# Ten modulation slices of the first attention, accumulated on GpSimd and not on VectorE

## The chip, the core and the metric

One core of a Trainium2 chip. The time is the device time of one execution in microseconds. A core has TensorE (matmuls and transposes, into PSUM), VectorE, ScalarE and GpSimd (elementwise work), and SyncE, whose queue issues the DMA transfers here. Each engine works through its own instructions in order; they meet at semaphores.

## What is computed

A decoder trunk of two layers on 512 positions of width 1024, float32. Layer 0 mixes positions with a forgetting attention of 16 heads, layer 1 with a latent attention; a gated MLP with a short convolution follows each. Every one of the four sub-layers is modulated by a vector c:

```python
def ada_modulation(c, w, b):
    mod = jax.nn.silu(c) @ w + b            # w: 1024 x 3072
    shift, scale, gate = jnp.split(mod[:, None, :], 3, axis=-1)
    return shift, scale, gate
...
    shift, scale, gate = ada_modulation(c, ada_w[i, 0], ada_b[i, 0])
    h = rms_norm(x) * (1.0 + scale) + shift
    ...
    x = x + gate * y
```

The change concerns silu(c) @ w alone, for the gate of sub-layer 0 and the shift and scale of sub-layer 1.

## The kernel before

**Products.** Activations lie transposed: a tile has 128 features on partitions and 512 positions in the row. A weight block of 128 output features is loaded to raw (8 x 128 columns), one of two slots. To keep float32 accuracy it is split: ScalarE copies it to wh in a reduced format (L711), VectorE subtracts to get the rest, wl (L1134). A product is then 24 matmuls of 512 columns (L1679): high times high, low times high, high times low, for 8 blocks of depth, into one of two PSUM banks pj. SyncE loads the next block of a slot when L1134 has read the one before (slot_free, L483). A bank is free for TensorE when both ScalarE and VectorE have taken the result that it held (bank_free).

**Head pairs.** The first attention goes over 8 pairs of heads. Steps are numbered i, w: i = 0 to 3, w = 0 to 7, each i two pairs, each pair four steps d = w mod 4, one for each block of 128 queries, with d + 1 blocks of keys. In a step TensorE makes the scores of both heads (L1918 to L1924), then a part of the next pair's q, k and v products as filling, transposes the probabilities of the step before (L1934), and fills again; v is transposed once a pair (L2027), and at d = 0 the pair before is weighted (L1962). VectorE takes the row maxima (L1297), ScalarE the exponentials (L861, into tmp or diag), VectorE the reciprocals (L1305) and the normalisation (L1307). The scores of a step wait for the exponentials of the step before, since they use the same two banks sc. Behind that VectorE has: at d = 0 the split of one block and a half of v's copy (L1276), which frees the bank in which the k product starts six matmuls into the next step; at d = 1 the copy of v's transposes (L1326), the low part of the pair's output (L1312), a split and the low part of q (L1265); at d = 2 a split and the low part of k (L1271). In the last i the pairs run out, w = 4 to 7 have less filling, taken from the output projection.

**Modulation.** The vector-matrix product is done row by row: partitions hold rows of w, each is multiplied by its silu(c), and slices of rows are added up; a matmul with ones sums over partitions in the end (ada_sum, L1799 and L1802). A slice p is 1 MB, 2048 columns on 128 partitions of ada_w_sb, which has two halves used in turn. ADA is the list of slices: 0 to 3 are the gate of sub-layer 0 (each with two row blocks of 1024 columns and two values of c), 4 to 11 the shift and scale of sub-layer 1. The load of slice p (L499) overwrites slice p - 2 and waits until slice p - 1 has been added to it (ada_acc); after a sum it waits for the sum. Its place in SyncE's queue is written by hand (FOX_ADA_LOAD, FOXO_ADA_LOAD). The accumulation, ada_step, is one instruction of VectorE for 2048 columns, or two for 1024: multiply by c and add the slice before (L1175), or multiply alone for the first of a sum (L1177). Its place in VectorE's order is the table FOX_ADA, in which n is 8 i + w: slices 0 to 9 stand behind the steps n = 3, 7, 10, 12, 15, 19, 22, 24, 27 and 31. Slices 10 and 11 stand in the output projection. The gate's sum is taken by TensorE at i = 1, w = 6, the other in the output projection.

**GpSimd** builds constants at the start and then has nothing until 671 us, where it works out shift sums for the second layer (L680, L685).

Of the kernel before, what the change touches and what calls it, by code (L numbers as in the profile page):

```python
# [10 lines left out]
ALU = mybir.AluOpType  # L11
# [69 lines left out]
GK = AW // D  # L81
# [4 lines left out]
ADA = tuple((is_gate, k, g, DT // GK if is_gate else DT) for is_gate, k in ADA_GROUPS  # L86
            for g in range(DT // GK if is_gate else DT))
ADA_END = tuple(sum(DT // GK if is_gate else DT for is_gate, _ in ADA_GROUPS[:n + 1])
                for n in range(len(ADA_GROUPS)))
ADA_OUT = {0: ADA_END[1] - 2, 3: ADA_END[1] - 1}  # L90
# [7 lines left out]
LAST_FILL = (0, 4, 8, 11, 14, 17, 19, 20, 21, 22, 24, 33)  # L98
MLA_FILL = (0, 3, 7, 11, 15, 18, 21, 33, 33)
OUT_SUM = {5: 1}  # L100
FOX_ADA = {(n // 8, n % 8): p for p, n in enumerate((3, 7, 10, 12, 15, 19, 22, 24, 27, 31))}
FOX_ADA_LOAD = {(0, 5): 2, (1, 2): 3, (1, 3): 4, (1, 5): 5, (2, 2): 6, (2, 5): 7}
FOXO_ADA_LOAD = {0: 8, 2: 9, 3: 10, 4: 11}

# [35 lines left out]
def build(nc, x, c, ada_w, ada_b, fox_w_in, fox_b_f, fox_w_o, mla_w_a, mla_g_q, mla_g_kv,  # L140
# [7 lines left out]
    with ExitStack() as ctx:  # L148
        def sb(name, shape, dt):
            return ctx.enter_context(nc.sbuf_tensor(name, shape, dt))  # L150

        def sem(name):
            return ctx.enter_context(nc.semaphore(name))
# [19 lines left out]
        ada_w_sb = sb("ada_w_sb", [P, 2, AW], F32)  # L173
# [12 lines left out]
        csil = sb("csil", [P, DT], F32)  # L186
# [165 lines left out]
        x_e = sem("x_e")  # L352
        ada_in = [sem(f"ada_in{i}") for i in range(2)]
        ada_used = sem("ada_used")
        ada_acc = sem("ada_acc")
        ada0_in = [sem(f"ada0_in{i}") for i in range(BLOCKS)]
        f_in = sem("f_in")
# [93 lines left out]
        def ada_tiles(p):  # L451
            return ada_w_sb[:, p % 2, :].rearrange("p (t n) -> p t n", n=D)
# [194 lines left out]
        def _(pool):  # L647
# [19 lines left out]
            for part, row0 in enumerate((0, 32, HD + 1, HD + 33)):  # L667
                pool.wait_ge(pc, 7 + part)
                pool.affine_select(out=sel[:, :, :], in_=flags, compare_op=ALU.not_equal, fill=1.0,
                                   base=-row0, pattern=[[-2, PAIRS], [0, P]], channel_multiplier=1  # L670
                                   ).then_inc(pc, 1)

            def shift_sum(n0, side, k):

# [451 lines left out]
        def _(dve):  # L1126
# [38 lines left out]
            def ada_step(p):  # L1165

                is_gate, k, g, _ = ADA[p]
                dve.wait_ge(ada_in[p % 2], 16 * (p // 2 + 1))
                if g:
                    dve.wait_ge(ada_acc, p)  # L1170
                for t in range(GK if is_gate else 1):
                    w, was = [ada_tiles(q)[:, t, :] if is_gate else ada_w_sb[:, q % 2, :] for q in (p, p - 1)]
                    c_col = csil[:, g * GK + t:g * GK + t + 1] if is_gate else csil[:, g:g + 1]
                    if g:
                        ins = dve.scalar_tensor_tensor(out=w, in0=w, scalar=c_col, in1=was, op0=ALU.mult, op1=ALU.add)  # L1175
                    else:
                        ins = dve.tensor_scalar(w, w, c_col, None, ALU.mult)  # L1177
                ins.then_inc(ada_acc, 1)
# [160 lines left out]
            last = PAIRS // 2 - 1  # L1339
            for i in range(last):  # L1340
                for w in range(8):
                    fox_step(i, w, True, None)
                    if (i, w) in FOX_ADA:
                        ada_step(FOX_ADA[i, w])
            for w in range(9):
                fox_step(last, w, w < 4, 6 * last)
                if (last, w) in FOX_ADA:
                    ada_step(FOX_ADA[last, w])

            def xtile(m):  # L1350
                return xT[:, m, :] if isinstance(m, int) else xT[:, bass.ds(m, 1), :]
# [292 lines left out]
            last = HEADS // 2 - 1  # L1644
# [609 lines left out]
```

## Time and profile before

| | before |
|---|---|
| median of 3 runs | 1299.44 us (1298.76 to 1301.04) |
| the profiled execution | 1300.4 us |
| its span, first to last instruction | 1298.2 us |
| mean granted TensorE clock | 0.989 |
| TensorE busy | 1259.0 us (97%) |
| VectorE busy | 847.2 us (65%) |
| ScalarE busy | 540.2 us (42%) |
| GpSimd busy | 30.8 us (2%) |

The head pairs run from about 62 to 263 us. A busy share is an average over stages; what an edit is worth is read from the place where it stands. In a timeline a row has its start and its duration in us; "[0.68 <-ACT diag L861]" says that the engine sat idle 0.68 us before it and that line 861 of ScalarE released it.

### The profile page before, as it was taken

What the parts mean: (1) busy time and instruction counts of PE and PEld (TensorE: products, weight loads), DVE (VectorE), ACT (ScalarE), POOL (GpSimd) and SP (SyncE); (2) the same over time, 40 slices, a digit from 0 to 9 for tenths busy, and PEclk for the clock granted to TensorE, in tenths of its full rate; (3) what the DMA queues carried; (4) which work ended last, traced back from release to release, by engine and by line L of the source; (5) the groups of instructions that cost most, each with busy time, mean ns of one, the idle gap of its engine ahead of it and who ended that gap; (6) DMA issues with size and microseconds to landing.
All of it is one profiled execution on the core that took longest, in us unless ns stands there. A gap on an engine that the chain in (4) does not pass through costs nothing.

```text
span 1298.2 us, 17924 instructions
## 1 busy us (share of the span) xinstructions
PE 1259.0 (97%) x6179; PEld 984.7 (76%) x6179; DVE 847.2 (65%) x1284; ACT 540.2 (42%) x983; POOL 30.8 (2%) x39
## 2 busy tenths in 40 slices
PE   5999999999999999999999999999999999999997
PEld 3677777676888878888888666667788888888886
DVE  3656756766888888855547767765776666664332
ACT  5544444534333333332235566664543333332222
POOL 2000000000000000000020000000300000000000
PEclk8999999999999999999999999999999999999998
DMA  9623433342566656556532111123233333333332
GB/s 308 192 66 97 139 101 107 111 146 49 195 195 195 195 188 194 168 165 209 164 98 60 38 34 36 34 59 93 70 102 95 97 96 96 97 93 105 90 90 93
DMA packets 241012, 154.42 MB, mean 119 GB/s; under 512 B 38153, under 2 KB 232174, under 8 KB 237882
## 3 DMA queue, kind: packets, MB, share of 16 engines
q1 hardware_dynamic: 240954, 153.63, 39.6%
q8 instruction: 38, 0.62, 0.2%
q14 instruction: 20, 0.16, 0.0%
HBM read 151.47 MB, written 2.14 MB: 118 GB/s over the span
## 4 chain that ended last, share of the span: by engine, by line
PE 87%; DVE 6%; ACT 2%; SPq 2%; issue 1%; DMA 1%; POOL 0%; DVEq 0%; ACTq 0%; POOLq 0%
PE pj L1679 74%; PE ov L1962 3%; PE sc L1906 3%; PE tr L1934 3%; PE sc L1918 1%; DVE wl L1134 1%; SPq L530 1%; DVE tmp L1228 1%; ACT wh L711 1%; DMA first_ada<-in_ada_w_dram 1%; DVE nmax L1297 1%; PE ov L1847 1%; DVE hl L1209 0%; PE sc L1924 0%; ACT tmp L861 0%
## 5 line engine op out<-in xcount | busy, mean ns | idle before, releaser
L1134 DVE TENSOR_TENSOR wl<-raw,wh 128x1024 fp32r<-128x1024 f32 (+2 forms) x214 | 236.1, 1103 | 264.2 <-ACT wh L711 261.0
L711 ACT ACTIVATE wh<-raw 128x1024 fp32r<-128x1024 f32 (+2 forms) x214 | 204.4, 955 | 456.8 <-PE pj L1679 456.8
L1679 PE MATMUL pj<-hh,wh 128*128 128x512 f32 x944 | 377.0, 399 | 6.4 <-issue 3.1
L1679 PE MATMUL pj<-hh,wl 128*128 128x512 f32 x944 | 368.2, 390 | 0.0
L1679 PE MATMUL pj<-hl,wh 128*128 128x512 f32 x944 | 367.8, 390 | 0.0
L1679 PE MATMUL pj<-gh,wh 128*128 128x512 f32 x560 | 223.0, 398 | 1.1 <-DVE rope_sb L1597 0.5
L1679 PE MATMUL pj<-gh,wl 128*128 128x512 f32 x560 | 219.3, 392 | 0.0
L1679 PE MATMUL pj<-gl,wh 128*128 128x512 f32 x560 | 218.7, 391 | 0.0
L1679 PEld LDWEIGHTS pj<-hh,wh 128*128 128x128 f32 x944 | 177.4, 188 | 48.7 <-issue 10.2
L1679 PEld LDWEIGHTS pj<-hh,wl 128*128 128x128 f32 x944 | 177.3, 188 | 37.8
L1679 PEld LDWEIGHTS pj<-hl,wh 128*128 128x128 f32 x944 | 177.6, 188 | 33.6 <-DVE hl L1209 0.2
L1679 PEld LDWEIGHTS pj<-gh,wh 128*128 128x128 f32 x560 | 105.5, 188 | 27.7 <-issue 6.0
L1679 PEld LDWEIGHTS pj<-gh,wl 128*128 128x128 f32 x560 | 105.3, 188 | 22.1
L1679 PEld LDWEIGHTS pj<-gl,wh 128*128 128x128 f32 x560 | 105.4, 188 | 20.1
L1297 DVE TENSOR_REDUCE nmax<-sc 128x1 f32<-128x128 f32 (+3 forms) x128 | 59.4, 485 | 43.4 <-PE sc L1907 27.2
L861 ACT ACTIVATE tmp<-sc,nmax 128x128 f32<-128x128 f32 (+2 forms) x96 | 46.7, 488 | 94.9 <-DVE nmax L1297 94.9
L1175 DVE SCALAR_TENSOR_TENSOR ada_w_sb<-ada_w_sb,csil 128x1024 f32<-128x1024 f32 (+1 forms) x45 | 78.9, 1776 | 0.0
L868 ACT ACTIVATE soft<-tr 128x128 f32<-128x128 f32 (+3 forms) x128 | 52.5, 438 | 63.0 <-PE tr L1934 62.2
L1433 DVE SCALAR_TENSOR_TENSOR tmp<-pj,conv,tmp 128x510 f32<-128x510 f32 x84 | 62.9, 748 | 7.0 <-DVE tmp L1430 1.4
L967 ACT ACTIVATE tmp<-pj,conv 128x512 f32<-128x512 f32 x84 | 64.0, 762 | 0.0
L1430 DVE SCALAR_TENSOR_TENSOR tmp<-pj,conv,tmp 128x511 f32<-128x511 f32 x84 | 62.5, 744 | 0.0
L1906 PE MATMUL sc<-soft 128*128 128x128 f32 (+3 forms) x128 | 47.1, 449 | 0.9 <-DVE soft L1606 0.7
(216 smaller groups left out, 1048.2 us busy)
## 6 DMA issues: line engine op xcount, KB each, us to landing
raw<-in_ffn_w_in_dram SPq DMA_DIRECT2D x88, 512.0 KB, 3.8
ada_w_sb<-in_ada_w_dram SPq DMA_DIRECT2D x40, 1024.0 KB, 5.2
raw<-in_ffn_w_out_dram SPq DMA_DIRECT2D x32, 448.0 KB, 3.4
raw<-in_fox_w_in_dram SPq DMA_DIRECT2D x24, 512.0 KB, 3.8
first_ada<-in_ada_w_dram SPq DMA_DIRECT2D x16, 512.0 KB, 8.9
raw<-in_ffn_w_out_dram SPq DMA_DIRECT2D x16, 512.0 KB, 3.6
raw<-in_fox_w_o_dram SPq DMA_DIRECT2D x8, 512.0 KB, 3.7
raw<-in_mla_w_o_dram SPq DMA_DIRECT2D x8, 512.0 KB, 3.7
```

What stands on the lines that cost most here:

```text
L711: act.activation(wh[:, n0 % 2, 0:kt, :], raw[:, n0 % 2, 0:kt, :], ACT.Copy).then_inc(w_hi, 1)
L861: act.activation(prob[u % 4][:, 0:nc_], SC[u % 2][:, 0:nc_], ACT.Exp, bias=nmax[:, u % 8:u % 8 + 1], accum_out=rsum[:, u % 8:u % 8 + 1]).t ...
L868: act.activation(pt32(h, b), TR[bk][:, 0:(b + 1) * P].rearrange("p (k q) -> p k q", q=P), ACT.Copy).then_inc(p_out, 1)
L967: act.activation(y, PJ[(T + j) % 2][:, :], ACT.Identity, bias=ccol(l, 3, f), scale=ccol(l, 2, f)).then_inc(ev_a, 1)
L1134: dve.tensor_tensor(wl[:, n0 % 2, 0:kt, :], raw[:, n0 % 2, 0:kt, :], f32(wh[:, n0 % 2, 0:kt, :]), ALU.subtract).then_inc(w_lo, 1)
L1175: ins = dve.scalar_tensor_tensor(out=w, in0=w, scalar=c_col, in1=was, op0=ALU.mult, op1=ALU.add)
L1297: dve.tensor_reduce(nmax[:, u % 8:u % 8 + 1], SC[u % 2][:, 0:nc_], AX.X, ALU.max, negate=True).then_inc(nmax_s, 1)
L1430: dve.scalar_tensor_tensor(out=y[:, 1:S], in0=bk[:, 0:S - 1], scalar=ccol(l, 1, f), in1=y[:, 1:S], op0=ALU.mult, op1=ALU.add).then_inc(tap, 1)
L1433: dve.scalar_tensor_tensor(out=y[:, 2:S], in0=bk[:, 0:S - 2], scalar=ccol(l, 0, f), in1=y[:, 2:S], op0=ALU.mult, op1=ALU.add).then_inc(ev_ ...
L1679: ins = pe.matmul(bank_[:, :], (wl if term == 2 else wh)[:, s, kt, :], (rl if term == 1 else rh)(kt), start=start and j == 0, stop=stop an ...
L1906: pe.matmul(sc, q32(par)[:, q], k32(par)[:, 0:nc_], start=True, stop=False)
L1934: ins = pe.transpose(TR[bk][:, kb * P:(kb + 1) * P] if h == 0 else TR[bk][:, (b - kb) * P:(b - kb + 1) * P], prob[u % 4][:, kb * P:(kb + 1 ...
```

## The change

The table FOX_ADA and its calls of ada_step are gone from VectorE. GpSimd has a loop over slices 0 to 9 right behind its constants. For each it waits for the slice to land, multiplies it in place (one instruction, or two of 1024 columns), waits for that to be finished and for the slice before, and adds that one in a second instruction. The semaphores to SyncE and TensorE are the same. Slices 10 and 11 and all later ones stay with VectorE.

```diff
-FOX_ADA = {(n // 8, n % 8): p for p, n in enumerate((3, 7, 10, 12, 15, 19, 22, 24, 27, 31))}
...
+        ada_mul = sem("ada_mul")
...
+            def ada_slice(p):
+
+                is_gate, k, g, _ = ADA[p]
+                pool.wait_ge(ada_in[p % 2], 16 * (p // 2 + 1))
+                for t in range(GK if is_gate else 1):
+                    w = ada_tiles(p)[:, t, :] if is_gate else ada_w_sb[:, p % 2, :]
+                    c_col = csil[:, g * GK + t:g * GK + t + 1] if is_gate else csil[:, g:g + 1]
+                    ins = pool.tensor_scalar(w, w, c_col, None, ALU.mult)
+                if not g:
+                    ins.then_inc(ada_acc, 1)
+                    return
+                ins.then_inc(ada_mul, 1)
+                pool.wait_ge(ada_mul, sum(ADA[q][2] > 0 for q in range(p + 1)))
+                pool.wait_ge(ada_acc, p)
+                pool.tensor_tensor(ada_w_sb[:, p % 2, :], ada_w_sb[:, p % 2, :], ada_w_sb[:, (p - 1) % 2, :], ALU.add
+                                   ).then_inc(ada_acc, 1)
+
+            for p in range(ADA_END[1] - len(ADA_OUT)):
+                ada_slice(p)
...
                 for w in range(8):
                     fox_step(i, w, True, None)
-                    if (i, w) in FOX_ADA:
-                        ada_step(FOX_ADA[i, w])
             for w in range(9):
                 fox_step(last, w, w < 4, 6 * last)
-                if (last, w) in FOX_ADA:
-                    ada_step(FOX_ADA[last, w])
```

VectorE around step n = 10 (d = 2) and the maxima of n = 11, before: ada_w_sb is the slice, csil is silu(c), nmax the row maxima.

```order
120 L1134 TENSOR_TENSOR wl<-raw,wh 128x1024 [waits w_hi]
121 L1271 TENSOR_TENSOR gl<-pj,gh 128x512 [waits ev_a]
122 L1175 SCALAR_TENSOR_TENSOR ada_w_sb<-ada_w_sb,csil 128x1024 [waits ada_acc,ada_in0]
123 L1175 SCALAR_TENSOR_TENSOR ada_w_sb<-ada_w_sb,csil 128x1024
124 L1297 TENSOR_REDUCE nmax<-sc 128x1 [waits score] x2
```

The same place after; the line numbers of VectorE's code have grown by 20.

```order
116 L1154 TENSOR_TENSOR wl<-raw,wh 128x1024 [waits w_hi]
117 L1291 TENSOR_TENSOR gl<-pj,gh 128x512 [waits ev_a]
118 L1317 TENSOR_REDUCE nmax<-sc 128x1 [waits score] x2
119 L1325 RECIPROCAL rinv<-rsum 128x1 [waits expd]
120 L1327 TENSOR_SCALAR tmp<-tmp,rinv 128x512 [waits rinv_s]
```

The two halves of slice 2 are gone from between the low part of k and the maxima.

GpSimd behind its constants, before: the next work is that of 671 us.

```order
17 L664 AFFINE_SELECT mask_b<-mask_b 128x128
18 L669 AFFINE_SELECT sel<-sel 128x1024 [waits pc] x4
19 L680 TENSOR_TENSOR tmp<-raw,mod 128x1024 [waits raw_in0,mod_ok]
20 L685 TENSOR_TENSOR tmp<-tmp 128x512 [waits c_acc]
21 L685 TENSOR_TENSOR tmp<-tmp 128x256 [waits c_acc]
```

After, the first three slices there (ada_in0 and ada_in1 are the landings in the two halves).

```order
18 L669 AFFINE_SELECT sel<-sel 128x1024 [waits pc] x4
19 L680 TENSOR_SCALAR ada_w_sb<-ada_w_sb,csil 128x1024 [waits ada_in0]
20 L680 TENSOR_SCALAR ada_w_sb<-ada_w_sb,csil 128x1024
21 L680 TENSOR_SCALAR ada_w_sb<-ada_w_sb,csil 128x1024 [waits ada_in1]
22 L680 TENSOR_SCALAR ada_w_sb<-ada_w_sb,csil 128x1024
23 L687 TENSOR_TENSOR ada_w_sb<-ada_w_sb 128x2048 [waits ada_acc,ada_mul]
24 L680 TENSOR_SCALAR ada_w_sb<-ada_w_sb,csil 128x1024 [waits ada_in0]
25 L680 TENSOR_SCALAR ada_w_sb<-ada_w_sb,csil 128x1024
26 L687 TENSOR_TENSOR ada_w_sb<-ada_w_sb 128x2048 [waits ada_acc,ada_mul]
```

The slices stand in one run with no other work between them; what spaces them is the landing of each.

## Rows read from the trace of the kernel before

**Rows 1.** The page: busy us (share) xinstructions of each engine; the chain that ended last.

```profile
PE 1259.0 (97%) x6179; PEld 984.7 (76%) x6179; DVE 847.2 (65%) x1284; ACT 540.2 (42%) x983; POOL 30.8 (2%) x39
...
PE 87%; DVE 6%; ACT 2%; SPq 2%; issue 1%; DMA 1%; POOL 0%; DVEq 0%; ACTq 0%; POOLq 0%
```

**Rows 2.** Waits of TensorE, 80 to 290 us: us in total, times, longest.

```profile
PE sc L1918 <- ACT diag L861: 1.5, 2, 0.8
```

**Rows 3.** Timeline of VectorE, 210 to 216 us: start us, us, line, operation.

```profile
211.76 2.34 DVE L1175 SCALAR_TENSOR_TENSOR ada_w_sb<-ada_w_sb,csil 128x2048 f32<-128x2048 f32 x1
214.02 1.28 DVE L1297 TENSOR_REDUCE nmax<-sc 128x1 f32<-128x512 f32 x2
```

**Rows 4.** Timeline of TensorE at three places; in brackets its idle time before.

```profile
55.60 0.39 PE L1679 MATMUL pj<-hh,wh 128*128 128x512 f32 x1
...
216.33 0.33 PE L1918 MATMUL sc<-gh 64*128 64x128 f32 x2 [0.68 <-ACT diag L861]
...
254.72 0.50 PE L1918 MATMUL sc<-gh 64*128 64x512 f32 x2 [0.44 <-ACT tmp L861]
```

**Rows 5.** Timeline of GpSimd, 671 to 676 us.

```profile
671.78 1.90 POOL L680 TENSOR_TENSOR tmp<-raw,mod 128x1024 f32<-128x1024 f32 x1 [662.95 <-DMA raw<-in_mla_w_a_dram]
673.76 2.84 POOL L685 TENSOR_TENSOR tmp<-tmp 128x512 f32<-128x512 f32 x2
```

**Rows 6.** Timeline of VectorE, 671 to 681 us.

```profile
671.85 2.78 DVE L1134 TENSOR_TENSOR wl<-raw,wh 128x896 fp32r<-128x896 f32 x1 [1.62 <-ACT wh L711]
674.55 1.25 DVE L1154 TENSOR_TENSOR mod<-mod_in,cols 128x8 f32<-128x8 f32 x1
...
680.30 0.75 DVE L1361 SCALAR_TENSOR_TENSOR xT<-pj,mod,xT 128x512 f32<-128x512 f32 x1 [1.90 <-PE pj L1679]
```

**Rows 7.** Timeline of VectorE, 53 to 56 us.

```profile
53.43 1.22 DVE L1134 TENSOR_TENSOR wl<-raw,wh 128x1024 fp32r<-128x1024 f32 x1 [3.14 <-ACT wh L711]
54.57 0.69 DVE L1265 SCALAR_TENSOR_TENSOR gl<-pj,gh 128x512 fp32r<-128x512 f32 x1
```

**Rows 8.** GpSimd by shape: three short stretches, then the span; busy us, mean ns.

```profile
L685 POOL TENSOR_TENSOR tmp<-tmp 128x512 f32<-128x512 f32 x1 | 2.0, 2022 | 0.1
...
L685 POOL TENSOR_TENSOR tmp<-tmp 128x512 f32<-128x512 f32 x1 | 1.3, 1285 | 0.1
...
L685 POOL TENSOR_TENSOR tmp<-tmp 128x256 f32<-128x256 f32 x1 | 0.7, 733 | 0.1
...
L669 POOL TENSOR_SCALAR_AFFINE_SELECT sel<-sel 128x1024 fp32r<-128x1024 f32 x4 | 4.4, 1092 | 0.6
```

**Rows 9.** Groups of VectorE by shape, whole span.

```profile
L1307 DVE TENSOR_SCALAR diag<-diag,rinv 128x512 f32<-128x512 f32 x24 | 11.7, 487 | 0.8
...
L1660 DVE TENSOR_SCALAR ada_w_sb<-tr,stat 128x512 f32<-128x512 f32 x1 | 0.7, 743 | 0.0
```

**Rows 10.** Timeline of SyncE's DMA queue, loads of a slice.

```profile
41.53 0.39 SPq L499 DMA_DIRECT2D ada_w_sb<-in_ada_w_dram  x1
...
159.40 0.35 SPq L499 DMA_DIRECT2D ada_w_sb<-in_ada_w_dram  x1
```

**Rows 11.** Line 499, issues of 35 to 280 us.

```profile
DMA to landing us min/median/max: 4.8/5.1/7.3
```

**Rows 12.** DMA issue of 159 to 160 us: count, KB, us to landing.

```profile
ada_w_sb<-in_ada_w_dram SPq DMA_DIRECT2D x1, 1024.0 KB, 5.9
```

**Rows 13.** Timeline of VectorE at later places of the head pairs.

```profile
170.50 0.42 DVE L1276 COPY tmp<-pj 128x256 f32<-128x256 f32 x1
...
236.67 1.23 DVE L1134 TENSOR_TENSOR wl<-raw,wh 128x1024 fp32r<-128x1024 f32 x1 [0.87 <-ACT wh L711]
...
238.42 1.28 DVE L1297 TENSOR_REDUCE nmax<-sc 128x1 f32<-128x512 f32 x2
...
250.35 0.35 DVE L1307 TENSOR_SCALAR tmp<-tmp,rinv 128x256 f32<-128x256 f32 x1
```

**Rows 14.** Chain of waits, 168 to 176 us: start us, us, what.

```profile
172.93 2.14 PE pj L1679 x9
```

## Prediction

> **What bounds the kernel now.** I read the views in this order. First the page's busy line and the chain that ended last: TensorE is busy for 97% of the span and 87% of the chain is TensorE [rows 1]. So an edit on another engine counts only where TensorE stands still for it, or comes to do so. Next who TensorE waits for in the stretch of the head pairs, 80 to 290 us: the largest line is 1.5 us in two waits for the exponentials of diag [rows 2]. Next the timelines around one of those two: on VectorE the slice of L1175 runs from 211.76 and the row maxima only from 214.02 [rows 3], the exponentials follow, and TensorE idles 0.68 us before the scores of 216.33 [rows 4]. That is what VectorE's slices cost today. Last, GpSimd's few rows late in the program, since there the two engines that the change makes neighbours already work side by side [rows 5, 6].
>
> **What those late rows show.** GpSimd starts a two-input operation at 671.78 and ends it at 673.68 [rows 5]. VectorE's L1134 (both inputs in SBUF, 896 columns) starts at 671.85 and takes 2.78 us, where even 1024 columns take 1.22 elsewhere [rows 6, 7]. It was held until GpSimd's instruction ended. The sequel goes on in turns: GpSimd's next one, issued at 673.76 while L1134 worked, takes 2.02 us where its like takes 1.29 [rows 8], and VectorE's 8-column addition of 674.55, two SBUF inputs, takes 1.25 us, until that one ends [rows 6]. L1361, with one input in PSUM, ran in 0.75 us beside GpSimd at 680.30 [rows 6]. So whole instructions exclude one another, whoever comes first goes first, and only VectorE operations of some kinds are concerned. The attention has two such kinds: L1134, and L1307, the normalisation. L1307 is one-input and SBUF to SBUF; it takes 0.49 us for 512 columns where the same operation reading PSUM takes 0.74 [rows 9], so it fetches two elements at a time, which needs the second path as two inputs do. No row shows it beside GpSimd. I take it as held; the case that it is not is a rival below. The Trainium skill has this rule on its page "SBUF — State Buffer", section "Who interferes with whom": VectorE and GpSimd share one pair of ports, taken for whole instructions, by two-SBUF-input operations and by one-input ones in a two-port mode. On L1134 the trace agrees (2.78 us against 1.22); on L1307 no run here shows it.
>
> **The change, part by part.**
>
> (1) Removed from VectorE: ten slices. Two of them, those right ahead of four-block maxima, make TensorE wait: minus 1.5 us [rows 2]. The other eight lie in VectorE's idle time. Where the two waits go, TensorE's own matmuls are next. The short last steps have waits too, but the slice there comes after them; they stay.
>
> (2) Added to GpSimd: 4 x 2 multiplications of 1024 columns, 6 of 2048, and 8 additions of 2048 columns. The additions: 128x256 takes 733 ns and 128x512 takes 1285 [rows 8], so 2.16 ns a column, and 2048 columns make 1.29 + 1536 x 0.00216 = 4.6 us, an estimate. The multiplications have no row. Below, the one-input select of 1024 columns takes 1.09 us [rows 8]; above, the two-input one of 1024 takes 1.90 us [rows 5]. I take the nearer kind: 1.1 us for 1024 and 2.1 for 2048. A slice is then some 6.8 us against 2.5 on VectorE, ten are about 60 us, and GpSimd has nothing else here. TensorE waits for finished slices only at the two sums, of which the first stands two head-pair steps behind the fourth slice's addition and the second behind slices that VectorE still does, so GpSimd's own slowness costs nothing. The Trainium skill's page "GPSIMD Engine Reference", section "4.1 Engine selection", calls one-input work there roughly line-rate; no run here shows that.
>
> (3) What GpSimd does to VectorE. Each slice holds VectorE's held kinds up to 2.1 us and then up to 4.6. GpSimd starts when a slice lands, not where the hand-written order had room.
>
> The start. Slice 1 is asked for at 41.53 and lands up to 7.3 us later, 48.8 [rows 10, 11]. Two multiplications and the addition, 2.3 + 4.7 us with their gaps, end at 55.8 at the soonest; I take 56.2, with one short turn left to VectorE between them. VectorE's L1134 of 53.43 is held until then, and behind it in the queue stands L1265, which frees the bank that TensorE writes from 55.60 on [rows 4, 7]. L1265 ended at 55.26 and now ends at 56.2 + 1.14 + 0.69 = 58.0. TensorE waits: **plus 2.4 us**.
>
> The steps with one block of keys (d = 0). Slices 2, 3, 5, 6 and 7 land as such a step begins. Slice 5, with all times 0.8 us earlier for the wait removed ahead of it: issue 159.40 - 0.8 = 158.6, landing 5.9 later [rows 10, 12], 164.5, multiplication to 166.6, one L1307 of 0.3, addition 166.9 to 171.5. The second L1307 is held until then and ends at 171.8, L1134 at 173.0, the copy L1276 at 173.4; it stood at 170.50 [rows 13]. TensorE needs the bank that this copy frees six matmuls (1.4 us) into the product of 172.93 [rows 14], less 0.8: at 173.5. It fits by 0.1; the other four come out at 0.1 to 0.6. I count **0.3 us** for all five, since small errors of mine can only add. Slice 4 is a multiplication alone and ends inside the slack.
>
> The last pair but one. Slice 8 is asked for behind a weight load that waits for the L1134 that slice 7 holds, at about 225.3; by 5.1 us to land [rows 11] it is ready about 230.3, and its addition runs about 233.8 to 238.4. The second L1307 of that step, L1134 (236.67 less 1.5 before) and the maxima (238.42 less 1.5) queue up behind it: the maxima start at 240.6, 3.7 us late [rows 13]. The slack of such a place: a slice of 2.34 us made a wait of 0.68 [rows 3, 4], so 1.65. The wait is 3.7 - 1.65 = 2.0 at most, and nothing if L1307 slips in ahead; I take **plus 1.8 us**.
>
> The last, short steps. Slice 9 is asked for at about 240.5, lands about 245.7, multiplies to 247.8, lets one L1134 pass, and its addition runs about 249.0 to 253.6. L1307 of 250.35 [rows 13] is held until then, 3 us of which 0.5 are covered because all stands 0.5 us later by now (-1.5 + 0.3 + 1.8, rounded), and the maxima of the next step stand behind it. TensorE already waits there, 0.44 us at 254.72, so no slack is left [rows 4]: **plus 2.5 us**.
>
> (4) The DMA queue. The slices are asked for earlier where SyncE waited for VectorE; weight loads behind them gain or lose 3 us and none is waited for. Nothing.
>
> Sum: -1.5 + 2.4 + 0.3 + 1.8 + 2.5 = +5.5 us. The profiled execution took 1300.4 us (span 1298.2, and 2.2 around it), so 1305.9; it lies 1.0 above the median of the runs, so **1305.0 us** there.
>
> **The rivals.**
>
> No exclusion that matters, which would not be slower: additions slip between VectorE's held operations, as L1361 ran beside GpSimd [rows 6]. Only -1.5 stays: 1297.9 us. Against it are the 2.78 and 1.25 us [rows 6]. It decides if slice 1's addition begins after the L1134 of 53.43 and the later maxima stay within 1.65 us of their places.
>
> L1307 is not held, only L1134: the start still costs 2.4; slice 8's addition then ends at 238.0 and holds the L1134 of 236.67 - 1.5 until there, the maxima come 2.8 late, a wait of 1.1 over the slack; slice 9 costs 0.2. -1.5 + 3.7 = +2.2: 1301.6 us. By the rule of the Trainium skill named above L1307 is held, and the time is the forecast's.
>
> Slow multiplications, 1.90 us for 1024 columns and 3.8 for 2048, as the two-input row [rows 5]. The same working with these gives: the start costs 4.0, the copies of the five one-block steps overshoot by 0.9, 0.6, 1.3, 1.1 and 1.6, and the last two slices about 6: 15.5 - 1.5 = +14: 1313 us.
>
> **How the numbers follow.** 0.2% is 2.6 us, about what a measurement of this kernel can tell from no change; the bounds are 1296.8 and 1302.0. Forecast 0.54 (1301 to 1309), L1307 free 0.15, no exclusion 0.12, slow multiplications 0.14, anything else 0.05. Faster: 0.04, the lower edge of the third. Same: 0.08 + 0.12 + 0.08 for the forecast's lower edge = 0.28. Slower: 0.68. The range of 8 in 10 takes in the third case's 1297.9 and stops within the slow one: 1297.5 to 1311.
>
> **What would show it.** Right: GpSimd busy some 60 us more; additions near 4.6 us and multiplications near 1.1 and 2.1; L1307 and L1134 with single instances of 3 to 5 us; TensorE idle 2.4 us near 55.6 for VectorE, nothing at 137 and 216, and 1.5 to 2.5 us near 239 and 254. Wrong: L1307 never longer than 0.5 us beside an addition; multiplications of 2 us and more; slice 1 landing after 50.6, since its addition would then begin behind L1134 of 53.43 and the start cost nothing.

## The result, and the profile after

The changed kernel takes **1316.67 us** (median of 4 runs, 1314.81 to 1320.67) where the kernel before, run on the same chip beside it, takes 1300.22. The ratio is 1.0135 (95% interval 1.0118 to 1.0153): slower by 16.5 us between the medians, 17.5 by the ratio. The forecast of 1305.0 had the direction, but the time lies above its range of 1297.5 to 1311.0. The profiled execution took 1314.81 us (span 1313.0); it is the fastest of the four, so the traces show some 15 us of the loss.

The page of the changed kernel, its busy line and the chain that ended last, answers to [rows 1]:

```profile
PE 1267.1 (97%) x6179; PEld 989.5 (75%) x6179; DVE 866.2 (66%) x1270; ACT 539.9 (41%) x983; POOL 123.8 (9%) x61
...
PE 83%; DVE 9%; ACT 3%; SPq 2%; issue 1%; DMA 1%; POOL 0%; DVEq 0%; ACTq 0%; POOLq 0%
```

GpSimd is busy 93 us more, not the 60 of the forecast. VectorE has ten slices less to do and is nevertheless busy 19 us longer, and its share of the chain goes from 6 to 9%: its instructions became longer. TensorE does the same matmuls and is busy 8 us longer.

GpSimd's groups by shape (busy us, mean ns of one), where [rows 8] had only other work:

```profile
L687 POOL TENSOR_TENSOR ada_w_sb<-ada_w_sb 128x2048 f32<-128x2048 f32 x8 | 36.7, 4590 | 0.7
L680 POOL TENSOR_SCALAR ada_w_sb<-ada_w_sb,csil 128x2048 f32<-128x2048 f32 x6 | 32.7, 5449 | 57.1 <-DMA ada_w_sb<-in_ada_w_dram 57.1
```

Its timeline has the smaller multiplications, undisturbed, in pairs:

```profile
116.72 5.67 POOL L680 TENSOR_SCALAR ada_w_sb<-ada_w_sb,csil 128x1024 f32<-128x1024 f32 x2 [57.30 <-DMA ada_w_sb<-in_ada_w_dram]
```

The additions are what the forecast said, 4.59 us. A multiplication of 2048 columns takes 5.45 us where 2.1 was assumed, and one of 1024 takes 2.83 where 1.1 was assumed. The multiplication, with one tensor as input, is slower than the addition of two.

TensorE's waits, 35 to 310 us (us in total, times, longest), answer to [rows 2], and the timeline of TensorE at five places to [rows 4]:

```profile
PE tr L1950 <- DVE soft L1346: 3.3, 1, 3.3
PE sc L1934 <- ACT diag L881: 2.9, 2, 1.6
PE sc L1934 <- DVE gl L1291: 2.7, 1, 2.7
PE sc L1934 <- ACT tmp L881: 0.9, 1, 0.9
```

```profile
64.37 0.33 PE L1934 MATMUL sc<-gh 64*128 64x128 f32 x2 [2.69 <-DVE gl L1291]
...
66.10 0.63 PE L1695 MATMUL pj<-hh,wh 128*128 128x512 f32 x1
...
168.76 0.33 PE L1934 MATMUL sc<-gh 64*128 64x128 f32 x2 [1.22 <-ACT diag L881]
...
248.49 0.33 PE L1934 MATMUL sc<-gh 64*128 64x128 f32 x2 [1.63 <-ACT diag L881]
...
266.87 0.69 PE L1950 MATMUL tr<-ident,diag 128*128 128x128 f32 x2 [3.34 <-DVE soft L1346]
```

Behind the first wait a 128x512 product takes 0.63 us; in [rows 4] it takes 0.39. (Products overlap: those of 0.39 us follow each other by 0.23, those of 0.63 by 0.43.) The table of stretches says why. Its columns are the stretch, its length, then busy time and count of PE, PEld, DVE, ACT and POOL, the granted clock, the DMA share and GB/s; first the changed kernel, then the kernel before:

```profile
64.00:83.00 19.00, 18.63 (x98) 14.53 (x100) 9.76 (x25) 8.15 (x22) 0.00 (x0) 0.91 0.30 84
...
238.00:256.00 18.00, 15.68 (x78) 11.14 (x78) 14.57 (x21) 8.54 (x22) 9.99 (x3) 0.83 0.38 122
256.00:279.00 23.00, 18.30 (x105) 11.57 (x102) 13.12 (x22) 7.41 (x22) 9.99 (x2) 0.84 0.22 69
```

```profile
64.00:83.00 19.00, 19.00 (x107) 14.75 (x106) 12.47 (x27) 9.28 (x24) 0.00 (x0) 1.00 0.30 84
...
238.00:256.00 18.00, 17.46 (x116) 12.32 (x115) 13.04 (x30) 8.95 (x27) 0.00 (x0) 1.00 0.37 118
256.00:279.00 23.00, 21.55 (x107) 16.39 (x106) 15.99 (x20) 8.87 (x15) 0.00 (x0) 1.00 0.45 148
```

The granted clock was at its 2.4 GHz level throughout these stretches before, and spent part of each at 1.2 GHz after.

The start of the scores of a head-pair step is a good milestone, since both kernels have 32 of them (steps 0 to 31). After minus before: +4.35 us at step 1, level until 11, +3.5 at 12 and +4.6 at 24 (a removed wait each, of 0.87 and 0.75), up by 1.5 at 16 (the wait of 168.76) and 0.3 at 19, to +6.2 at 28, +9.9 at 29 and +14.6 at 31. From there on nothing more is lost within a microsecond. So **four tenths of the loss lie in the first 28 steps and six tenths in the last three.**

On VectorE, this is what made it so, in the place of [rows 13] (start us, us, line). Line 1327 is the normalisation that was L1307, L1154 was L1134, L1302 was L1282:

```profile
56.00 3.96 DVE L1302 TENSOR_TENSOR tmp<-tmp 16x512 f32<-16x512 f32 x1 [0.76 <-ACT tmp L845]
...
158.88 5.40 DVE L1327 TENSOR_SCALAR tmp<-tmp,rinv 128x384 f32<-128x384 f32 x1
...
241.23 4.43 DVE L1154 TENSOR_TENSOR wl<-raw,wh 128x1024 fp32r<-128x1024 f32 x1 [0.88 <-ACT wh L731]
...
261.71 4.51 DVE L1327 TENSOR_SCALAR diag<-diag,rinv 128x256 f32<-128x256 f32 x1
```

And GpSimd in the same places:

```profile
42.56 12.15 POOL L680 TENSOR_SCALAR ada_w_sb<-ada_w_sb,csil 128x1024 f32<-128x1024 f32 x4 [33.73 <-DMA ada_w_sb<-in_ada_w_dram]
54.80 4.61 POOL L687 TENSOR_TENSOR ada_w_sb<-ada_w_sb 128x2048 f32<-128x2048 f32 x1
...
158.62 5.45 POOL L680 TENSOR_SCALAR ada_w_sb<-ada_w_sb,csil 128x2048 f32<-128x2048 f32 x1 [5.66 <-DMA ada_w_sb<-in_ada_w_dram]
...
240.87 5.45 POOL L680 TENSOR_SCALAR ada_w_sb<-ada_w_sb,csil 128x2048 f32<-128x2048 f32 x1 [6.89 <-DMA ada_w_sb<-in_ada_w_dram]
...
261.54 4.53 POOL L687 TENSOR_TENSOR ada_w_sb<-ada_w_sb 128x2048 f32<-128x2048 f32 x1
```

Lay the two over each other. The normalisation of 158.88 ends at 164.28, the multiplication that began 0.26 us ahead of it ends at 164.07. L1302 ends at 59.96, the addition at 59.41. The last one ends at 266.22, its addition at 266.07. Each of these VectorE instructions ends 0.15 to 0.6 us behind GpSimd's, so it was held for as long as that one ran. The third is different. L1154 of 241.23, with two inputs, ends at 245.66, and the multiplication beside it only at 246.32. L1154 takes 1.22 us of its own, so it was let go at about 244.4, 1.9 us before the multiplication's end. All six instances of L1154 that a multiplication holds in this trace end 0.65 us before it does, and the one of 53.41, begun 1.3 us before a multiplication's end, takes 1.23 us, no longer than alone. So **a multiplication holds the one-input L1327 to its end, and the two-input L1154 only up to 1.9 us before it.**

### The profile page after: what moved, and what is told of

Same layout as the page of the kernel before. It is cut to its first block, busy times and chain, and to the rows that moved or that the text cites. A ratio compares the mean times of both kernels' runs of the same rounds, so it can differ in the third digit from the quotient of the medians.

```text
span 1313.0 us, 17932 instructions
## 1 busy us (share of the span) xinstructions
PE 1267.1 (97%) x6179; PEld 989.5 (75%) x6179; DVE 866.2 (66%) x1270; ACT 539.9 (41%) x983; POOL 123.8 (9%) x61
## 4 chain that ended last, share of the span: by engine, by line
PE 83%; DVE 9%; ACT 3%; SPq 2%; issue 1%; DMA 1%; POOL 0%; DVEq 0%; ACTq 0%; POOLq 0%
PE pj L1695 71%; PE ov L1978 3%; PE sc L1922 3%; PE tr L1950 2%; DVE wl L1154 2%; PE sc L1934 1%; DVE tmp L1327 1%; SPq L530 1%; DVE tmp L1248 1%; ACT wh L731 1%; DMA first_ada<-in_ada_w_dram 1%; DVE nmax L1317 1%; DVE hl L1229 1%; ACT tmp L881 1%; DVE diag L1327 0%
## 5 line engine op out<-in xcount | busy, mean ns | idle before, releaser
L1154 DVE TENSOR_TENSOR wl<-raw,wh 128x1024 fp32r<-128x1024 f32 (+2 forms) x214 | 244.5, 1143 | 262.2 <-ACT wh L731 259.1
L680 POOL TENSOR_SCALAR ada_w_sb<-ada_w_sb,csil 128x1024 f32<-128x1024 f32 (+1 forms) x14 | 56.2, 4022 | 163.7 <-DMA ada_w_sb<-in_ada_w_dram 163.7
L700 POOL TENSOR_TENSOR tmp<-raw,mod 128x1024 f32<-128x1024 f32 x4 | 9.6, 2402 | 603.7 <-DMA raw<-in_mla_w_a_dram 423.0
```

What stands on the lines that cost most here:

```text
L680: ins = pool.tensor_scalar(w, w, c_col, None, ALU.mult)
L1154: dve.tensor_tensor(wl[:, n0 % 2, 0:kt, :], raw[:, n0 % 2, 0:kt, :], f32(wh[:, n0 % 2, 0:kt, :]), ALU.subtract).then_inc(w_lo, 1)
```

## The experiments

The theory after this reading: while one whole GpSimd instruction runs, it holds VectorE instructions of the kinds above; the price of the multiplication was wrong, so each hold is longer than in the forecast and more places have no slack for it; the waits that follow let TensorE's clock fall, which costs again. The rivals: the price alone is not it and another term is wrong; GpSimd's finished slices come too late for somebody; the slow matmuls have another cause than TensorE's idleness. Each run is compared with the kernel before on the same chip (1299.1 to 1299.4 us in these).

Start of the scores of three steps in each profiled execution (us) and the median time:

| kernel | step 1 | step 28 | step 31 | time | ratio to before (95%) |
|---|---|---|---|---|---|
| before | 66.62 | 242.27 | 254.72 | | |
| changed | 70.97 | 248.49 | 269.29 | 1316.67 | 1.0118 to 1.0153 |
| one column | 66.09 | 240.04 | 252.49 | 1296.77 | 0.9972 to 0.9990 |
| all in pieces | 66.95 | 240.91 | 253.35 | 1308.46 | 1.0060 to 1.0088 |
| multiplications in pieces | 66.22 | 241.51 | 257.65 | 1302.58 | 1.0019 to 1.0051 |
| additions in pieces | 70.28 | 249.06 | 266.10 | 1307.09 | 1.0041 to 1.0072 |
| slices 0, 1 on VectorE | 66.10 | 250.61 | 267.12 | 1313.79 | 1.0098 to 1.0129 |
| slices 8, 9 on VectorE | 72.81 | 248.21 | 260.66 | 1304.23 | 1.0026 to 1.0052 |
| multiplications at the assumed price | 68.77 | 245.64 | 259.80 | 1304.72 | 1.0028 to 1.0059 |
| fills in place of both | 67.17 | 241.12 | 253.57 | 1297.24 | 0.9973 to 0.9992 |
| idle products, late | 72.50 | 248.77 | 269.80 | 1316.18 | 1.0111 to 1.0142 |
| idle products, in the wait | 69.53 | 251.73 | 270.47 | 1313.44 | 1.0086 to 1.0119 |
| pieces, slice 9 on VectorE | 66.95 | 240.91 | 253.41 | 1297.78 | 0.9977 to 0.9995 |

### One column: what is the gain without GpSimd's work

```diff
-                    ins = pool.tensor_scalar(w, w, c_col, None, ALU.mult)
+                    ins = pool.tensor_scalar(w[:, 0:1], w[:, 0:1], c_col, None, ALU.mult)
```

The addition likewise.

> Edit: GpSimd's multiplications and additions of slices 0 to 9 work on the first column alone (the other 2047 columns of each slice stay as loaded, so the modulation is not the reference's); loads, waits, semaphores and the order stay. Theory H (holding: each whole GpSimd instruction keeps VectorE's operations with two SBUF inputs, or of the fast one-input kind, waiting until it ends; nothing else costs): only the removed slices are left of the change, so 1.5 us under the kernel before, 1298 to 1299.5 us, with no wait of TensorE at the scores behind the four-block maxima of slices 2 and 6. Rival L (lateness: what costs is that a slice is finished 8 us later, so loads behind it in SyncE's queue and the sums come late): the same here, since a one-column slice is done at once. If it stays above 1305 us, neither holds and the loss lies in the order or the handshakes.

Measured 1296.77 us, ratio 0.9981: minus 2.4 us. So all waits, loads and semaphores of the change are harmless, and what makes it slow is how long GpSimd works. The gain that the forecast put at 1.5 us is 2.4, with an interval (1.3 to 3.6 us) that takes in the 1.5. At the two waits 1.7 goes; 0.5 more is there before step 1, which these executions differ by anyway.

### Pieces: are whole instructions what holds

```diff
+                    for a in range(0, D if is_gate else AW, 256):
+                        ins = pool.tensor_scalar(w[:, a:a + 256], w[:, a:a + 256], c_col, None, ALU.mult)
```

Multiplications and additions both, then multiplications alone, then additions alone.

> Edit: the same multiplications and additions on GpSimd, cut into pieces of 256 columns, 8 and 8 for a slice, nothing else. Theory H: no piece holds VectorE longer than 0.9 us (from 2.56 and 2.16 ns a column and 0.2 us each), which the slack of nearly every step covers: 1298 to 1302 us, VectorE's L1134 and L1307 of the code before never over 2.2 us, and no low clock behind the first scores. Rival L: a slice takes even longer, some 13 us and not 10, so 1316 us or more. Rival S (the two engines share a rate, so that the sum of GpSimd's work counts and not the length of an instruction): as the changed kernel or slower, 1316 to 1322 us.

> Edit: only the multiplications are cut into pieces of 256 columns, the additions of 2048 columns stay whole. Theory H: what is left is the holding by 4.6 us of addition, that is about what the prediction summed up for it, 1302 to 1308 us; single VectorE operations of up to 5 us while an addition runs and of up to 1.7 us while multiplications run. Rivals L and S: 1316 us or more.

> The changed kernel with the additions in pieces of 256 columns and the multiplications whole, the counterpart of the run with the multiplications in pieces (1302.6 us). If the whole multiplications (2.95 and 5.45 us each) are what holds VectorE at the waits that count from slice 4 on, the time stays close to the changed kernel: the start's 2.7 us and the clock behind it are recovered, the rest not, which gives 1310 to 1315 us. If additions were the larger share, it comes down to 1303 to 1306 us.

With both in pieces GpSimd does more work (by shape: 256 columns, busy us, mean ns), and the head pairs lose nothing: step 31 comes 1.4 us earlier than in the kernel before.

```profile
L681 POOL TENSOR_SCALAR ada_w_sb<-ada_w_sb,csil 128x256 f32<-128x256 f32 x80 | 80.8, 1029 | 128.0 <-DMA ada_w_sb<-in_ada_w_dram 128.0
L690 POOL TENSOR_TENSOR ada_w_sb<-ada_w_sb 128x256 f32<-128x256 f32 x64 | 53.6, 871 | 0.7
```

134 us of GpSimd's work in instructions of about 1 us cost the head pairs nothing, where 93 us in instructions of up to 5.4 us cost them 14.6. It is the length of one instruction that counts, not the sum. Yet the kernel took 1308.46 us, where 1298 to 1302 had been expected. The reason is one wait behind the head pairs, in the timelines of VectorE, GpSimd and SyncE's queue:

```profile
277.18 2.35 DVE L1198 SCALAR_TENSOR_TENSOR ada_w_sb<-ada_w_sb,csil 128x2048 f32<-128x2048 f32 x1 [8.62 <-DMA ada_w_sb<-in_ada_w_dram]
```

```profile
264.90 7.04 POOL L690 TENSOR_TENSOR ada_w_sb<-ada_w_sb 128x256 f32<-128x256 f32 x8
```

```profile
271.96 0.34 SPq L499 DMA_DIRECT2D ada_w_sb<-in_ada_w_dram  x1
```

Slice 9 is done at 271.94. Only then is slice 10's load issued, since slice 9's addition reads the buffer that it fills. VectorE stands before slice 10 with the residual additions of the output projection queued behind it, and TensorE waits 8.1 us for them. So lateness is a second cost, real as soon as pieces make a slice 14 us long; in the changed kernel with whole instructions (slice 9 done at 266.07, all of TensorE's steps late as well) it did not show.

Multiplications alone in pieces gave 1302.58 us (seven of eight executions within 0.5 us, one at 1311.18), additions alone 1307.09. I had expected 1310 to 1315 for the latter, if the multiplications were nearly all of it. They aren't: additions of 4.6 us hold too. I had also expected the start to be recovered there, and it was not: step 1 is 3.7 us late. The trace of that run is its slowest execution, 1310.85 us, so its step 31 is later than that of a typical one. With the multiplications in pieces, slice 8's addition (245.10 to 249.67) held VectorE, in its timeline, and step 30 came 1.9 us late:

```profile
245.91 4.84 DVE L1156 TENSOR_TENSOR wl<-raw,wh 128x1024 fp32r<-128x1024 f32 x1 [1.72 <-ACT wh L733]
```

Against the run with one column, both whole cost 20 us, more than the sum of the additions alone (6 to 7) and the multiplications alone (10). A likely reason, not tested, is that a multiplication and an addition in a row leave VectorE one short turn between them.

### The assumed price: was the rest of the sum right

```diff
+                    n = 348 if is_gate else 738
-                    ins = pool.tensor_scalar(w, w, c_col, None, ALU.mult)
+                    ins = pool.tensor_scalar(w[:, 0:n], w[:, 0:n], c_col, None, ALU.mult)
```

> The changed kernel, but each GpSimd multiplication works on 348 of its 1024 columns or 738 of its 2048, so that one takes about the 1.1 or 2.1 us of the prediction (part of the modulation is left unscaled, so the output is not the reference's; all loads, waits and additions stay as they are). It asks whether the price of the multiplication alone was the wrong term. If so, the sum of the prediction comes out: about 1305 us, between 1301.5 and 1308.5, with the first scores' wait of 2.7 us still there (the addition of slice 1 still holds VectorE), the granted clock back at 1.00 from 238 us on, and the last scores 3 to 6 us later than in the kernel before, not 15. If other terms were wrong as well (additions that hold a short step cost more than 2.5 us, or the clock falls all the same), it stays at 1310 us or above.

Measured **1304.72 us**, where the prediction said 1305.0, with multiplications of 1.18 and 2.16 us:

```profile
L681 POOL TENSOR_SCALAR ada_w_sb<-ada_w_sb,csil 128x738 f32<-128x738 f32 x6 | 13.0, 2158 | 72.1 <-DMA ada_w_sb<-in_ada_w_dram 72.1
...
L681 POOL TENSOR_SCALAR ada_w_sb<-ada_w_sb,csil 128x348 f32<-128x348 f32 x8 | 9.4, 1183 | 115.6 <-DMA ada_w_sb<-in_ada_w_dram 115.6
```

The timelines of VectorE and TensorE at the start show the mechanism of the prediction, at its place and nearly its size. The addition ran from 51.25 to 55.85:

```profile
53.06 3.87 DVE L1156 TENSOR_TENSOR wl<-raw,wh 128x1024 fp32r<-128x1024 f32 x1 [2.91 <-ACT wh L733]
56.85 0.68 DVE L1287 SCALAR_TENSOR_TENSOR gl<-pj,gh 128x512 fp32r<-128x512 f32 x1
```

```profile
57.63 0.47 PE L1697 MATMUL pj<-hh,wh 128*128 128x512 f32 x1 [2.22 <-DVE gl L1287]
```

The milestones of this run against the kernel before give each term: start 2.15 us (2.4 said), the two removed waits 0.88 and 0.75 (1.5), the one-block steps 1.2 together (0.3), slice 8 1.6 (1.8), slice 9 1.7 (2.5). So the total is closer than its terms, since an error of 0.9 us one way and several the other way nearly cancel. The granted clock stayed at 1.00 from 64 us to the end of the head pairs.

### Ends of the loss: slices 0 and 1, slices 8 and 9

```diff
-            for p in range(ADA_END[1] - len(ADA_OUT)):
+            for p in range(ADA_END[1] - len(ADA_OUT) - 2):
```

Slices 8 and 9 go back to VectorE behind steps 27 and 31; in the other run slices 0 and 1 behind steps 3 and 7.

> Edit: slices 0 and 1 are back on VectorE behind the steps n = 3 and n = 7 as before, slices 2 to 9 stay on GpSimd. Theory H: the 3.3 us by which the addition of slice 1 holds the sum of the forget gate, the wait of 2.7 us before the first scores and the low clock behind it go, about 5 us: 1310 to 1313 us. If the loss at the start came from something else in the changed kernel (transfers, code), it stays at 1315 us or more.

> The changed kernel with its last two slices, 8 and 9, back on VectorE where the kernel before has them (behind steps 27 and 31); slices 0 to 7 stay on GpSimd with whole instructions. The anchors put 9.3 us of the changed kernel's 15.5 between steps 28 and the end, and about 6 ahead of it. If that stretch is lost to GpSimd's work on slices 8 and 9 and to the clock behind the waits it causes, the granted clock is 1.00 from 238 to 279 us, steps 29 to 31 come 4.5 to 6.5 us later than in the kernel before, and the time is 1303.5 to 1306.5 us. If the end's loss comes from the lateness gathered before, it stays above 1310 us.

With 0 and 1 back, step 1 comes at 66.10 us, the start's 4.9 us all recovered, but the time falls by only 2.9. TensorE's waits of that run show where the rest was given back, at later transposes that wait for the normalisation:

```profile
PE tr L1954 <- DVE tmp L1329: 6.6, 4, 4.1
```

With 8 and 9 back, the median falls by 12.4 us, and the stretch is whole again:

```profile
238.00:279.00 41.00, 39.00 (x226) 28.24 (x225) 30.50 (x55) 18.71 (x48) 0.00 (x0) 1.00 0.37 119
```

I had written that the milestones put 9.3 us there. In the traces step 31 comes 8.6 us earlier than in the changed kernel, although step 1 comes 1.8 us later, so the two slices carry some 10 us in the traces and 12.4 by the medians. The later step 1 is the clock's doing: the code up to there and the wait (2.68 us, ended at 64.78) are the same, but products of 0.63 us run until 71.2 us in place of 68.7, and the granted clock from 64 to 83 us is 0.82, not 0.91. **The same wait cost 1.4 us of slow products in one execution and 2.9 in the other.** The lateness at step 28 is 5.9 us in this run too, and the whole kernel ends 5.1 late, so with VectorE on time at the end nothing is added.

### Idle products: does the clock fall for idleness

```diff
             taps()
+            pe.wait_ge(pc, 11)
+            idle_products(11)
             pe.wait_ge(cum_ok, 2)
-            pe.wait_ge(pc, 11)
```

They write the free score bank and change nothing. In a first run they stood one wait too late, and so began after 1.39 us of idleness:

> The changed kernel, and 11 idle 128x512 products into the free score bank just ahead of the first pair's scores, where TensorE waits 2.69 us for VectorE (at 0.23 us each they fill 2.5 us). They change nothing in what is computed. Theory that the slow matmuls behind the wait (0.63 us in place of 0.39, granted clock 0.91 in the 19 us) come from TensorE's idleness: the matmuls behind the first scores keep 0.39 us, the second step's scores come 1.5 to 2 us earlier than 70.97 us, and the time falls by that, to 1314.5 to 1315.3 us (some may be given back where GpSimd's fixed schedule holds VectorE later, so 0.5 to 2 us in all). Rival, that they are slow for another reason (the operands, VectorE's and GpSimd's work at the memory): they stay at 0.63 us and the time does not fall.

> The changed kernel, with the 11 idle 128x512 products right behind the transposes at 61.0 us, ahead of TensorE's first wait there (in the run before they stood behind a wait for the cumulated biases, started at 63.20 us and ran at 0.40 us each). Theory that the idleness brings the slow stretch: they run from about 61.8 us at 0.23 us each, the first scores start at 64.4 to 64.7 us, the products behind them take 0.39 and not 0.63 us, and the second step's scores start at 69.1 to 69.6 us in place of 70.97. The 1.4 to 1.8 us are there in the head pairs; of the whole, 0.3 to 1.8 us may be left, 1314.5 to 1316 us. Rival: the idle products themselves run at 0.40 us, and the second step's scores are no earlier.

The first placement missed: the timeline of TensorE has them 0.40 us apart, so the scores were pushed to 67.52 and only 0.5 us of time was gained, within the uncertainty:

```profile
63.20 4.39 PE L1790 MATMUL sc<-sel 128*128 128x512 f32 x11 [1.39 <-ACT cum L852]
```

It does show that the slow stretch starts even so: 1.39 us of waiting were enough here. In the second placement they fill the wait, 0.25 us apart:

```profile
61.77 2.80 PE L1790 MATMUL sc<-sel 128*128 128x512 f32 x11
64.54 0.33 PE L1935 MATMUL sc<-gh 64*128 64x128 f32 x2
...
66.69 0.40 PE L1695 MATMUL pj<-hh,wh 128*128 128x512 f32 x1
```

The products behind them take 0.40 us, not 0.63, the clock is at 1.00 from 64 to 83 us, and step 1 comes at 69.53, 1.44 us earlier. So idleness it is, and the operands and VectorE's work were the same. This was tested at the start alone. In the changed kernel the lateness grows by 10.0 us from step 27 to step 31; the waits there add up to 6.5 us, where the kernel before has 0.4, so the slow products can have cost up to 3.9 us, an estimate. What is left of the 1.44 us at the end is not settled: 1313.44 us is 3.2 below the changed kernel's median, but was measured beside other runs; in its profiled execution the span is 1313.9, TensorE waits 4.1 us at a place where the changed kernel waits less than 1, and step 31 is 1.2 us later.

### Fills: is it reading, writing, or just the length

```diff
-                    ins = pool.tensor_scalar(w, w, c_col, None, ALU.mult)
+                    ins = pool.memset(w, 0.0)
```

The addition likewise; nothing is read.

> GpSimd fills the slices with zeros in place of the multiplications and additions: it writes the same elements and reads none (the modulation of the first layer is lost, so the output is not the reference's). It asks whether VectorE is held by any GpSimd work on the memory or by work that reads it. If a fill holds VectorE like an addition does: L1327 instances beside a 128x2048 fill take over 1.5 us in place of 0.49, and the time lies above 1300 us. If only reads (or two operands) hold it: L1327 stays at 0.49 us and the time is that of the run with one column, 1296 to 1298 us.

Half of what I wrote came out. A fill of 2048 columns takes 1.81 us, one that began at 243.12 ended at 244.93, and VectorE was held by it and by the next:

```profile
243.00 2.00 DVE L1328 TENSOR_SCALAR tmp<-tmp,rinv 128x128 f32<-128x128 f32 x1
...
245.06 1.80 DVE L1328 TENSOR_SCALAR tmp<-tmp,rinv 128x128 f32<-128x128 f32 x1
```

128 columns take 0.29 us alone. So work that only writes holds the one-input kind just as well. The two-input kind it does not hold. In the timelines of VectorE and GpSimd, L1155 (the same split) runs wholly inside a fill and takes 1.22 us, its time alone:

```profile
230.48 1.22 DVE L1155 TENSOR_TENSOR wl<-raw,wh 128x1024 fp32r<-128x1024 f32 x1
```

```profile
230.32 1.82 POOL L688 MEMSET ada_w_sb<- 128x2048 f32 x1
```

Four more that began inside a fill (at 116.27, 142.15, 194.89 and 220.77) take 1.23 us each. The time was 1297.24 us, that of one column: holds of up to 2 us fit into the slack everywhere.

### Both costs taken away

GpSimd in pieces for slices 0 to 8, slice 9 back on VectorE behind step 31, so that slice 10's load goes out as early as in the kernel before.

```diff
+FOX_ADA = {(3, 7): 9}
...
-            for p in range(ADA_END[1] - len(ADA_OUT)):
+            for p in range(ADA_END[1] - len(ADA_OUT) - 1):
```

> GpSimd's multiplications and additions in pieces of 256 columns as in the run with both in pieces, and slice 9 given back to VectorE behind the last head pair's scores, where the kernel before has it (one fused instruction of 1.1 and 2.1 us). If the 8.6 us wait of VectorE for the load of slice 10 came from GpSimd finishing slice 9 at 271.9 us, the load goes out near 258 us, the wait is gone, and what is left is the gain of the eight or nine slices taken from VectorE: 1297 to 1299.5 us, ratio 0.998 to 1.000 to the kernel before. If pieces cost VectorE time that only looked free, or slice 10 waits for another reason, it stays above 1303 us.

Measured 1297.78 us, ratio 0.9986 (0.9977 to 0.9995): **faster than both kernels**, by 1.6 us (0.1%) against the kernel before; the interval excludes 1, if narrowly. Slice 10's load goes out at 259.99 in place of 271.96, the 8.6 us wait is gone, and TensorE has no wait above 1.2 us from 35 to 310. VectorE still pays for the pieces, out of its idle time: L1158 in its 22 instances of 64 to 256 us takes 1.29 us in the mean where the kernel before has 1.22.

```profile
L1158 DVE TENSOR_TENSOR wl<-raw,wh 128x1024 fp32r<-128x1024 f32 x22 | 28.4, 1291 | 24.9 <-ACT wh L735 24.9
```

## Why the prediction was wrong, step by step

The terms of its sum beside what the milestones give, in us. (Differences of steps' starts, one execution each; by the medians of the times the last two totals are 5.3 and 16.5.)

| term | said | at the assumed price | changed kernel |
|---|---|---|---|
| (1) the two removed waits | -1.5 | -1.6 | -1.6 |
| (3) the start | 2.4 | 2.2 | 4.4 |
| (3) the one-block steps | 0.3 | 1.2 | 0.3 |
| (3) slice 4 | 0 | 0 | 1.5 |
| (3) slice 8 | 1.8 | 1.6 | 5.4 |
| (3) slice 9 | 2.5 | 1.7 | 4.6 |
| together, at step 31 | 5.5 | 5.1 | 14.6 |

**What bounds the kernel: right.** Only places where TensorE stands still counted, and all of the loss lies in the head pairs.

**Exclusion of whole instructions, and L1307 as one of the held kinds: right.** The prediction had rows for L1134 alone and took L1307 by an argument; it was held 5.40, 4.00 and 4.51 us. The rule of the Trainium skill's page "SBUF — State Buffer", section "Who interferes with whom", holds for both kinds here, with a difference that the prediction left out. By that section a VectorE instruction with two SBUF inputs contends only with a GpSimd instruction that reads SBUF, and the fills agree (1.22 us beside one). The rule that one holder keeps the pair for a whole instruction is stated there for the two-port mode, and L1327 agrees (5.40 us, until the multiplication's end). The prediction took it over for L1154: that holds beside additions, but a multiplication let L1154 go 1.9 us before its end, and there the measurement decides. Two things more were left out. The exclusion also covers L1282 (now L1302), the 16-row difference of the biases with two SBUF inputs, and multiplications hold as well as additions: 5.40 us beside slice 4, which the prediction had called "a multiplication alone" that "ends inside the slack". It did not: TensorE waited 1.22 us at 168.76, and the step came 1.5 us later.

**(1) The removed slices: right, a little small.** Said 1.5; both waits are gone, 1.6 us in the milestones; the run with one column gained 2.4 (1.3 to 3.6).

**(2) The price of the multiplications: the step that failed.** "I take the nearer kind: 1.1 us for 1024 and 2.1 for 2048." They take 2.83 and 5.45. The upper bound taken from a two-input row, 1.90 and 3.8, was no bound either. A select with one input, [rows 8], is not like a multiplication by a column of scalars, and nothing in the rows made two inputs dearer than one input and a scalar per partition. The sentence that the slow case would give 1313 had the right sign of what was to come and a chance of 0.14; what 5.45 in place of 3.8 gives was not worked out. The Trainium skill's page "GPSIMD Engine Reference", section "4.1 Engine selection", calls one-input work there roughly line-rate; this case's rows say no, 5.45 us against 4.59 for the addition of the same shape. With the multiplications at the assumed price the kernel takes 1304.72 us against the 1305.0 forecast, and step 31 is 5.1 us late in place of 14.6: this price is what moved the time out of the range. The other terms were each off by up to 0.9 us and nearly cancelled, so that the total came within 0.3 us is partly luck.

**(3) The start: near in size, by another way, which is luck.** With multiplications of 3 us, slice 1's addition began at 54.80, behind L1134 of 53.43. The prediction's own condition said that then "the start cost nothing". It cost 2.69 us, because L1302 was next in line and was held; then the clock took 1.4 more, which the prediction had no term for. In the run at the assumed price the way was that of the prediction, 2.22 us for 2.4.

**(3) The one-block steps and slice 8:** 0.3 and 1.8 said, 1.2 and 1.6 at the assumed price. The estimates of 0.1 to 0.6 us to spare were too tight. In the changed kernel slice 8 cost 5.4: its multiplication already makes L1154 of 241.23 take 4.43 us, and its addition then holds L1327 of 247.91 for 3.32.

**(3) The last short steps: right place, too small.** 2.5 us were said for slice 9 and 4.6 measured; with slice 8 it is 4.3 against 10.0, or 12.4 by the medians. Waits of 1.6, 0.7, 3.3 and 0.9 us come one after the other, and the granted clock is 0.83 and 0.84 in the two stretches that hold them. The prediction had no term for the clock at all.

**(4) The queue: nothing, right for this kernel.** In pieces it becomes 8.6 us.

**The rivals.** No exclusion and L1307 not held are both refuted by VectorE's rows. Slow multiplications was the true case, its 1313 still 3.7 short. Even that is partly luck: it gave the one-block steps 5.5 us (they cost 0.3, and slice 4 1.5) and the last two slices 6 (they cost 10.0). It took every held instruction to wait for the multiplication's end, which L1154 does not, and had no clock.

## What to carry to other kernels

Moving work to GpSimd is paid in the length of its longest instruction, not in its sum: 134 us of pieces of 1 us were free where 93 us of instructions up to 5.4 us cost 15 (in the head pairs). Cut such work into pieces shorter than the slack of the VectorE instructions beside it, and then look who waits for the finished result, since pieces make it later. Which VectorE instructions are held depends on what GpSimd does: fills leave the two-input kind alone. If a price has no row, don't call the nearest kind's duration a bound; here the cheaper-looking form was the dearer one, and a chance of 0.14 on it was too little.

## What the runs showed of the hardware

On GpSimd a multiplication by a scalar per partition takes 2.83 us for 1024 columns and 5.45 for 2048, an addition of two tensors 4.59 for 2048, a fill 1.81. In pieces of 256 columns they take 1.03 and 0.87 beside VectorE's work. All three hold VectorE's one-input normalisation between SBUF tensors until they end (5.40 us beside a multiplication, 4.51 beside an addition, 2.00 beside a fill, against 0.3 to 0.5 alone). The two-input split of 1024 columns is held by an addition to its end (4.84 us in the run with the multiplications in pieces, against 1.22 alone), by a multiplication up to 1.9 us before its end, and by a fill not at all. A 2.7 us wait of TensorE was followed by matmuls of 0.63 us in place of 0.39 from 65.7 to 69 us, and 11 idle products in the wait kept them at 0.40; in another execution the same wait was followed by matmuls of 0.63 us from 66.6 to 71.2 us; a wait of 2.22 us at 57.63, in the run at the assumed price, was followed by no slow stretch from 64 us on, one of 1.39, ended at 63.20, was, and so was one of 1.15, ended at 63.69, in the run with the additions in pieces. Which waits let the clock fall stays open.
